# The first projection begins over half of its depth, and gate rows are spread by transfers through a line in DRAM

## The reference, cut to what matters

```python
mod = silu(c) @ w_mod[i] + b_mod[i]
sh1, sc1, g1, sh2, sc2, g2 = split(mod, 6)
h = rmsnorm(x, norm1_g) * (1 + sc1) + sh1
q, k, v, r = split(h @ w_in)          # gated linear attention, latents and context
x = x + g1 * y                        # gate 1
f = moe(rmsnorm(x, norm2_g) * (1 + sc2) + sh2)
x = x + g2 * f                        # gate 2
# second block: two layers (ab: two kinds of attention; cd: window attention and convolution)
h = rmsnorm(x) * (1 + scale) + shift
x = x + gate * mix(h)                 # a gate for latents, one for context in layer ab, one in layer cd
```

## Time and profile before

| | us |
|---|---|
| median of 3 runs | 1036.72 |
| lowest and highest run | 1036.17, 1038.57 |
| profiled execution, span from first to last instruction (it has no other time) | 1037.2 |
| TensorE matmuls busy | 953.9 |
| VectorE busy | 370.3 |
| ScalarE busy | 292.4 |
| GpSimd busy | 31.0 |

### The profile page before, as it was taken

The page is one execution under the profiler, slowest core; times in us unless marked ns, Lnnn a source line. Parts: engine busy times, 40 slices in busy tenths (PEclk is TensorE's granted clock), DMA queues, the critical chain, the costliest instruction groups (busy, mean ns, idle before and its releaser), DMA issues.

```text
span 1037.2 us, 11964 instructions
## 1 busy us (share of the span) xinstructions
PE 953.9 (92%) x4352; PEld 510.3 (49%) x4353; DVE 370.3 (36%) x876; ACT 292.4 (28%) x679; POOL 31.0 (3%) x53
## 2 busy tenths in 40 slices
PE   3899989999999889878877999999999999999998
PEld 1454446546444336323322655576454545676763
DVE  1200597624361000001000350485766423246452
ACT  3210543232322000000000341467666311225330
POOL 0100200000000000000000100000000000000000
PEclk8999999999999999999988999999999999999999
DMA  9955574489569999999999512205644104342411
GB/s 351 357 206 201 97 255 162 171 299 334 212 243 326 376 397 393 397 395 397 396 398 386 191 41 71 82 1 193 213 138 108 34 8 140 112 154 82 134 30 40
DMA packets 100750, 220.92 MB, mean 213 GB/s; under 512 B 2917, under 2 KB 5273, under 8 KB 100553
## 3 DMA queue, kind: packets, MB, share of 16 engines
q1 hardware_dynamic: 95520, 208.54, 55.9%
q0 software_dynamic: 2032, 6.84, 2.5%
q10 hardware_dynamic: 3128, 4.62, 1.2%
HBM read 214.48 MB, written 5.51 MB: 212 GB/s over the span
## 4 chain that ended last, share of the span: by engine, by line
PE 80%; DMA 8%; ACT 4%; SPq 3%; DVE 3%; issue 2%; ACTq 0%; DVEq 0%
PE bank L596 27%; PE bank L863 9%; PE bank L610 9%; DMA arena<-in_w_up_e_dram 5%; PE bank L876 4%; PE bank L893 4%; PE bank L1047 3%; PE bank L1066 3%; PE bank L562 3%; PE bank L888 3%; PE bank L1057 3%; DMA arena<-in_gla_w_in_dram 2%; SPq L1212 2%; PE bank L792 1%; SPq L1207 1%
## 5 line engine op out<-in xcount | busy, mean ns | idle before, releaser
L596 PE MATMUL bank<-arena 128*128 128x512 f32 (+3 forms) x672 | 269.9, 559 | 1.4 <-ACT arena L1443 0.7
L596 PEld LDWEIGHTS bank<-arena 128*128 128x128 f32 x672 | 125.9, 190 | 133.7 <-issue 124.1
L863 PE MATMUL bank<-arena 128*64 128x512 f32 x512 | 120.6, 625 | 13.1 <-issue 13.1
L610 PE MATMUL bank<-arena 128*128 128x256 f32 (+1 forms) x384 | 99.4, 417 | 4.0 <-DMA arena<-in_gla_w_in_dram 2.4
L610 PEld LDWEIGHTS bank<-arena 128*128 128x128 f32 x384 | 72.0, 190 | 32.2 <-issue 21.5
L863 PEld LDWEIGHTS bank<-arena 128*64 128x64 f32 x512 | 43.3, 144 | 87.0 <-issue 86.3
L876 PE MATMUL bank<-arena,con 128*64 128x512 f32 x272 | 62.1, 597 | 9.6 <-ACT con L1535 9.0
L562 PE MATMUL bank<-arena,silu_c 128*32 128x512 f32 x384 | 49.0, 633 | 8.4 <-DMA arena<-in_w_mod_dram 6.0
L1532 ACT ACTIVATE con<-bank 128x256 f32<-128x256 f32 x16 | 6.1, 384 | 177.6 <-PE bank L863 177.6
L2164 DVE TENSOR_TENSOR con<-con,bank 128x256 f32<-128x256 f32 x16 | 6.7, 420 | 135.4 <-ACT con L1532 135.4
L1047 PE MATMUL bank<-arena 64*128 64x512 f32 (+3 forms) x160 | 47.7, 545 | 2.2 <-ACT arena L1705 2.2
(11 more groups left out here) (351 smaller groups left out, 1067.7 us busy)
## 6 DMA issues: line engine op xcount, KB each, us to landing
arena<-in_w_gate_e_dram SPq DMA_DIRECT2D x16, 2048.0 KB, 20.0
arena<-in_w_up_e_dram SPq DMA_DIRECT2D x16, 2048.0 KB, 20.3
arena<-in_w_down_e_dram SPq DMA_DIRECT2D x16, 2048.0 KB, 19.8
arena<-in_w_mod_dram SPq DMA_DIRECT2D x12, 2048.0 KB, 11.8
arena<-in_mod_w_dram SPq DMA_DIRECT2D x12, 2048.0 KB, 8.5
arena<-in_gla_w_in_dram SPq DMA_DIRECT2D x6, 2048.0 KB, 10.8
arena<-in_ab_w_in_dram SPq DMA_DIRECT2D x6, 2048.0 KB, 16.4
arena<-in_cd_w_in_dram SPq DMA_DIRECT2D x6, 2048.0 KB, 7.8
```

Source lines behind the costliest of these rows:

```text
L596: mm = pe.matmul(ps[:, 0:n], lhs[:, k, tile * P:(tile + 1) * P], w[:, k, c0:c0 + n], start=(k == 0), stop=(k == kd_ - 1))
L610: mm = pe.matmul(ps[:, i * n:(i + 1) * n], w[:, k, c * P:(c + 1) * P], rhs[:, k, 0:n], start=(k == 0), stop=(k == KC - 1))
L863: mm = pe.matmul(up_b[64 * j:64 * j + 64, :], h[:, k, :], blocks[:, g + n:u + n + 1:u - g, :], start=(k == 0), stop=(k == KC - 1), tile_po ...
```

## The change

Two parts. **Front:** the chunks are made in the order 0, 2, 1, 3, so that after two of them shift and scale of the first four depth chunks are known. The key weights are loaded in two halves of the depth, the first behind the second modulation chunk, the second behind the fourth. TensorE turns depth chunks 0 to 3, and starts all four heads over that half, with modulation chunks and turns between; the four banks are held until the other half is added. **Gate rows:** the diagonals, matmuls and copies go; GpSimd's queue writes the columns as a line of 1024 values to DRAM, waits, and reads the line spread over the partitions.

```diff
+        gate_lines = nc.dram_tensor("gate_lines", [5, D], F32, kind="Internal").ap()
-        mod_chunks = [(0, c) for c in range(12)] + ...
+        mod_chunks = [(0, c) for c in (0, 2, 1, 3)] + [(0, c) for c in range(4, 12)] + ...
...
+            if m == 1:
+                for name, ks in (("k", slice(0, 4)), ("k_rest", slice(4, KC))):
+                    loads.append((name, [(slice(0, P), ks, cols_of(w_in, 512, 512)[:, ks, :])], 2, KC, 512))
+        loads.append(loads.pop(3))
-        FRONT_LOADS = [("k", 2), (4, 0), ("q", 1), (5, 0), ...
+        FRONT_LOADS = [(4, 0), ("q", 1), (5, 0), ...
...
-            for m in range(2):
-                mod(m)
-            turn(0, xn, range(0, 6))
-            banks.hold([f"turn0_{k}" for k in range(6)])
-            for m in range(2, 4):
-                mod(m)
+            mod(0)
+            turn(0, xn, range(0, 4))
+            mod(1)
             mod_flush()
+            def keys_part(h, ks):
+                w = weights(pe, "k")
+                if ks[0]:
+                    pe.wait_ge(k_rest_in, 16)
+                ps = banks.open(pe, f"k{h}", k_ready, h + 1) if ks[0] == 0 else banks.banks[banks.at[f"k{h}"][0]]
+                for k in ks:
+                    if h == 0:
+                        wait_turned(0, k)
+                    mm = pe.matmul(ps[:, :], w[:, k, h * P:(h + 1) * P], hT[:, k, :], start=(k == 0), stop=(k == KC - 1))
+                if ks[-1] == KC - 1:
+                    banks.filled(f"k{h}", mm)
+                    last_use["k"] = f"k{h}"
+            keys_part(0, range(0, 4))
+            keys_part(1, range(0, 4))
+            banks.hold(["k0", "k1"])
+            mod(2)
+            keys_part(2, range(0, 4))
+            banks.hold(["k2"])
+            mod(3)
+            turn(0, xn, range(4, 6))
+            mod_flush()
+            keys_part(3, range(0, 4))
+            banks.hold(["k3"])
+            turn(0, xn, range(6, KC))
             banks.give_back()
-            turn(0, xn, range(6, KC))
             for h in range(HG):
-                project_T(f"k{h}", "k", [h], 512, hT, k_ready, h + 1, turned=0 if h == 0 else None)
+                keys_part(h, range(4, KC))
                 if h == 1:
                     mod(4)
             mod(5)
...
-                if t == 0:
-                    gate(0)
...
-            ctx_latents(1)
-            gate(1)
-            ctx_latents(4)
+            ctx_latents(5)
+            pe.wait_ge(con_rest_in, 16)
             pe.wait_ge(routed, 1)
...
-                if m in AB_GATE_AT:
-                    gate(2 + AB_GATE_AT.index(m))
...
-            gate(4)
...
-            dve.wait_ge(gate_bc, 2)
+            dve.wait_ge(gate_row_in[0], 16)
...
+            def gate_row(u, col, targets):
+                line = gate_lines[u]
+                pool.dma_start(line.rearrange("(k p) -> p k", p=P), col, allow_slow_non_contiguous=True).then_inc(gate_line_out[u], 16)
+                pool.wait_ge(gate_line_out[u], 16)
+                for target, cs in targets:
+                    pool.dma_start(target, line[cs].partition_broadcast(target.shape[0])).then_inc(gate_row_in[u], 16)
+            pool.wait_ge(modcol_ready, 6)
+            gate_row(0, mod1[:, 16:24, 0], [(gate_rows[:, 0, :], slice(0, D))])
             banks.wait(pool, "z31")
...
+            pool.wait_ge(o_copied, 4)
+            pool.wait_ge(modcol_ready, 12)
+            gate_row(1, mod1[:, 40:48, 0], [(gate_rows[64 * h:64 * h + 64, 1, 0:512], slice(512 * h, 512 * h + 512))
+                                            for h in range(2)])
             banks.wait(pool, "col17")
...
+            pool.wait_ge(modcol_ready, 18)
+            pool.wait_ge(qk_ms, 8)
+            gate_row(2, mod2[:, 0, 16:24, 0], [(gate_rows[:, 0, :], slice(0, D))])
+            gate_row(3, mod2[:, 0, 16:24, 1], [(ctx_gate_row, slice(0, D))])
+            pool.wait_ge(modcol_ready, 24)
+            pool.wait_ge(y_added, 12)
+            gate_row(4, mod2[:, 1, 16:24, 0], [(gate_rows[:, 0, :], slice(0, D))])
```

More of the change, by code:

```diff
@@ L133, in hold @@
     def hold(self, names):
-        self.held = [self.at[x][0] for x in names]
+        self.held = self.held + [self.at[x][0] for x in names]
         self.order = [n for n in self.order if n not in self.held]
@@ L138, in give_back @@
         self.order += self.held
+        self.held = []
     def filled(self, name, ins):
@@ L328, in cols_of @@
             return w.rearrange("(k p) c -> p k c", p=P)[:, :, c0:c0 + n]
-        mod_chunks = [(0, c) for c in range(12)] + [(1, c) for c in range(6)] + [(2, c) for c in range(6)]
+        mod_chunks = [(0, c) for c in (0, 2, 1, 3)] + [(0, c) for c in range(4, 12)] + [(1, c) for c in range(6)] + [(2, c) for c in range(6)]
         w_in = a["gla_w_in"][0]
@@ L471, in build @@
         o_copied, o_rstd, o_ready, oT_ready = sem("o_copied"), sem("o_rstd"), sem("o_ready"), sem("oT_ready")
-        diag_gate, gate_bc, y_added = sem("diag_gate"), sem("gate_broadcast"), sem("y_added")
+        gate_line_out, y_added = [sem(f"gate_line{u}_out") for u in range(5)], sem("y_added")
+        gate_row_in = [sem(f"gate_row{u}_in") for u in range(5)]
         parts_zeroed, parts_copied = sem("parts_zeroed"), sem("parts_copied")
@@ L613, in project_T @@
                 last_use[wname] = name
[L615 to L630, removed]
             pe.wait_ge(con_in, 16)
@@ L1202, in fill @@
                 name, parts, s, kdim, n = ld
+                if name == "k_rest":
+                    rows, ks, src = parts[0]
+                    sp.dma_start(view(slot_at(s), kdim, n)[rows, ks, :], src).then_inc(k_rest_in, 16)
+                    return
                 if in_slot[s] is not None:
@@ L1316, in mod, with turn @@
                 act.activation(mod_rows[:, m % 2, :], ps[:, :], ACT.Copy).then_inc(row_ready, 1)
-            def turn(use, dst, cs, at=0):
-                act.wait_ge(coef_ready, max(c for _, _, c in cs) + 1)
-                for k in range(0, KC, 2):
+            def turn(use, dst, cs, at=0, ks=range(0, KC, 2), sem_=coef_ready):
+                act.wait_ge(sem_, max(c for _, _, c in cs) + 1)
+                for k in ks:
                     ps = banks.wait(act, f"turn{use}_{k}")
@@ L1326, in turn @@
                     ins.then_inc(turned_a, 1)
[L1328 to L1336, removed]
             act.wait_ge(cols_ready, 2)
@@ L1347, in _ @@
             norm(0, xn, arrived)
-            for m in range(4):
-                mod(m)
-            turn(0, hT, [(0, T, 0), (T, 512, 1)])
+            mod(0)
+            mod(1)
+            turn(0, hT, [(0, T, 0), (T, 512, 1)], ks=range(0, 4, 2), sem_=coef_first)
+            mod(2)
+            mod(3)
+            turn(0, hT, [(0, T, 0), (T, 512, 1)], ks=range(4, KC, 2))
             for h in range(HG):
@@ L1878, in turn @@
                     ins.then_inc(turned_v, 1)
-            def gate(u, col):
-                if u >= 1:
-                    banks.wait(dve, f"gate{u - 1}_1")
-                dve.tensor_tensor(gate_diag[:, :, :], outer(ident, KC), inner(col, P), ALU.mult).then_inc(diag_gate, 1)
             added = [0]
@@ L1902, in _ @@
             norm_rows(0, xn)
-            for m in range(4):
-                mod_col(m)
-            dve.wait_ge(modcol_ready, 4)
-            for m in range(2):
-                coefficients(m, mod1[:, 8:16, m], mod1[:, 0:8, m], column("norm1_g"))
-            turn(0, hT, [(0, T, 0), (T, 512, 1)])
+            for half, sem_ in ((0, coef_first), (1, coef_ready)):
+                mod_col(2 * half)
+                mod_col(2 * half + 1)
+                dve.wait_ge(modcol_ready, 2 * half + 2)
+                s4 = slice(4 * half, 4 * half + 4)
+                for m in range(2):
+                    coefficients(m, mod1[:, 8 + 4 * half:12 + 4 * half, m], mod1[:, 4 * half:4 * half + 4, m],
+                                 column("norm1_g")[:, s4], s4, sem_)
+                turn(0, hT, [(0, T, 0), (T, 512, 1)], ks=range(4 * half + 1, 4 * half + 4, 2), sem_=sem_)
             mod_col(4)
@@ L2390, in _ @@
             turn(5, hT, [(0, T, 5)])
-            gate(4, mod2[:, 1, 16:24, 0])
             for n, t in enumerate(CD_TILES):
```

43 lines of the change are left out of this document (18 added, 25 removed).

## The result

The change made the kernel slightly slower, by 0.2 to 0.4%. In the six runs beside six of the kernel before, the median is 1042.45 us (1038.68 to 1043.81) against 1037.09; ratio 1.0039, 95% interval 1.0028 to 1.0051. Twelve later runs of the same kernel (experiment 10) gave 1039.40 (1036.56 to 1041.96) and 1.0017 (1.0007 to 1.0028). The forecast was 1031.6, range 1030.0 to 1035.6. The profiled execution of the changed kernel took 1043.02 us with a span of 1041.2; in every run whose span is known the two differ by about 1.8. The runs of this document come in sets, from several chips, each with the kernel before beside it. One and the same kernel differed by up to 3.0 us from set to set (1042.45 and 1039.40 here), so a difference of that size between medians of different sets decides nothing.

What follows compares the result with a forecast made beforehand. TensorE's order was taken to bound the kernel, except the experts' stage, paced by the stream of weights. Front +0.8, second broadcast -0.7, third to fifth -5.16 sum to -5.1: median 1031.6 us, range 1030.0 to 1035.6.

Steps and rivals of the forecast that it cites:

- three signs: Forecast wrong if the gap's clock drops, the chunk after 715 waits for its load, or attention's turns begin no earlier.
- First broadcast, value 0: At 246.50, before the first output product: removal gains 0, since ScalarE's evictions still release the product at 248.60.
- rival 1: Clock falls in the 3.2 us gap before 248.60, slowing the product by 2.0: 1033.6; chance 0.22 alone.
- The line, 7.2 us and a stall of 0: After attention, near 697: each scattered line takes 7.2 us and delays the chunk wanted at 720.17 by 0.
- Rival 4: Scattered lines hold the DMA engines, making the chunk wanted at 720.17 late; up to 8.6 us, 1040.2; chance 0.07.
- Front, +0.8: Kernel start to the sixth chunk: the new order costs 0.8 us, bounds 0.4 to 1.8.
- the first two cases of the clock's rise: Front: clock rises at 25.8 as before, or 5.7 us after the restart; second chunk ends at 27.3 or 28.0.
- Rival 2: Clock falls in the front's 2.1 us gap before the first half of the keys, costing 2.0: 1033.6; chance 0.10 alone.
- Second broadcast, 0.7: Before the ranks' matmul at 296.11: removal gains 0.7 us, 0.55 sure, up to 1.0.
- Third to fifth, 5.16: Third, fourth (attention) and fifth broadcast: removal gains 1.72 us each, 5.16 together; upper bound 1.96 each.
- rival 3: ScalarE and VectorE set attention, so removing the third and fourth broadcast leaves holes: 2 x 1.72 less gain, 1035.0; chance 0.07.
- The experts' stage, "almost unmoved": The expert stage, paced by the stream of weights, begins +0.8 - 0.7 later, so almost unmoved.

Runs made afterwards that it cites:

- experiment 10: The whole change, unaltered, run once more beside the kernel before: 1039.40 us, ratio 1.0017.
- the pair: Whole change, third and fourth gate lines written at about 612 us, on one chip: with four throwaway matmuls in the first broadcast's gap 1032.36, without 1035.27.
- early lines: Against the whole change, third and fourth gate lines written to DRAM after the second context load, about 612 us: 1033.48, once more 1035.27.
- experiment 8: Front's edits alone, old gates, against 1037.25 before: unaltered 1040.69; sixth chunk in third chunk's buffer 1038.15; second chunk before first 16 transposes 1037.14.
- the rows alone, with early lines and fill: Gate rows by transfers, old front, third and fourth line written early, four throwaway matmuls in the first broadcast's gap: 1030.82, 0.9926 of the kernel before.

## Why the prediction was wrong

Two steps failed, and both are terms that the sum put at nothing: the line's stall of 0, which measured 7.30 us with the slow clock behind it, and the first broadcast's 0, which measured 2.95. Together they are 10.25 us. The forecast of -5.1 and the trace's +3.98 lie 9.0 apart: the front added 0.65 (1.45 at the first product, and not 0.8) and the second broadcast 0.2, while the other three broadcasts took 1.0 off and the experts' stage 1.06. Two of the three signs that the prediction named for its being wrong came: the clock dropped, and the chunk waited for its load.

**First broadcast, value 0: wrong.** That the product's start would not move was right (ScalarE's copies still release it). The step left out what the two matmuls did for the clock; it was kept apart as rival 1, at 2.0 us and 0.22. It happens in seven of eight profiles and makes the product up to 3.1 longer; the pair's medians differ by 2.9. The one wait that had stayed fast, of 2.43 us, was no guide to one of 3.18; the prediction's own rows had two falls, behind 2.23 and 2.9 us.

**The line, 7.2 us and a stall of 0: wrong, and the largest.** Rival 4 had the mechanism, at 0.07. The two lines took 10.4 to 13.2. The step's reason, that queues share the engines so that a load goes on beside a line, is what failed: the load moved at 6 to 32 GB/s. So did "only one of the two lines should meet that load": each waits for the one before it on GpSimd's queue, and both met it. The nearest rows were 1024 pieces of 64 bytes read from DRAM; 1024 pieces of 4 bytes written to it took 12.3 even in quiet, so the number of pieces alone doesn't set the time. The packet price of the Trainium skill, "DMA: Bandwidth & Descriptors", section "Measured", a figure for loads from DRAM, gave the prediction its estimate of 10.8 us; the 10.4 to 13.2 here lie about it, while the 3.0 of rows 9 for as many pieces doesn't fit it. The sum had not taken it.
Stall and slow clock cost 7.3 in the trace, 5.0 in the change's second profile; early lines took 4.1 to 9.0 off by the medians.

**Front, +0.8: mis-sized.** Its own bounds, 0.4 to 1.8, held in the trace (1.58), and each step was right to half a microsecond: second chunk's restart 25.1 forecast and 25.57 found, keys between 30.9 and 32.3 and found at 31.77, sixth chunk 68.0 to 69.4 and 69.14. The value lay between the first two cases of the clock's rise; the profile lies between the second and the third. By the medians the front costs 2.2 to 3.4; what makes up the rest is open (experiment 8). Rival 2 exists beside it: in three profiles with this front the first 16 half-depth passes took 8.80 us instead of 7.11. TensorE's timeline and stretches of one of them, the change's second profile (experiment 10):

```profile
21.65 3.63 PE L590 MATMUL bank<-con,arena 128*128 128x128 f32 x16 [5.20 <-DVE arena L1848]
25.21 1.92 PE L571 MATMUL bank<-arena,silu_c 128*32 128x512 f32 x16
...
30.56 8.80 PE L645 MATMUL bank<-arena 128*128 128x512 f32 x16 [2.05 <-ACT arena L1336]
```

```profile
29.00:31.00 2.00, 0.44 (x1) 0.30 (x2) 1.96 (x8) 1.61 (x4) 0.00 (x0) 1.00 1.05 388
31.00:36.00 5.00, 5.00 (x9) 2.11 (x8) 0.29 (x1) 0.33 (x1) 0.00 (x0) 0.66 1.05 387
```

The transposes, 0.23 us each, ran at the lower level and the second chunk at the higher; behind the gap of 2.05 the clock was still at 1.00 when the keys began, and fell after 31. There the sixth chunk is 2.30 late and not 1.58. Two readings of the prediction were off without touching its sum: the waits between 20.07 and 37.85 are 3.2 us and not about 4, and 1037.2 is a span, some 1.8 short of a time, so the profiled execution was 2.3 above the median of 1036.72 and not 0.5.

**Second broadcast, 0.7:** 0.50, about the part called sure.

**Third to fifth, 5.16: right in kind, too small.** 1.97 + 2.47 + 1.73 = 6.17, above the upper bound of three times 1.96. Besides the matmuls, short waits went: groups of TensorE in the stretch of the third and fourth of the kernel before,

```profile
L1057 PE MATMUL bank<-con,arena 128*128 128x128 f32 x60 | 8.5, 275 | 0.6 <-ACT arena L1705 0.5
```

and of the kernel with early lines,

```profile
L1068 PE MATMUL bank<-con,arena 128*128 128x128 f32 x60 | 8.1, 274 | 0.0
```

TensorE had waited 0.6 us at the turns, mostly for ScalarE, which had two evictions more to do there; that these are the cause is likely and not shown. The gain itself speaks against rival 3.

**The experts' stage, "almost unmoved":** 1.06 shorter in the change's profile. Since it varies by 3.9 between profiles without an edit in it, that can't be put down to the change; what sets it stays open.

With both faults repaired the forecast's reasoning about the broadcasts holds: the rows alone, with early lines and fill, are 7.4 us faster by the medians (1030.82 against 1038.17), of which the trace has 6.2 in the three large terms and 0.5 in the second.

## What to carry to other kernels

A step that idles an engine can be free for the order of work and still cost the clock: ask what ran in the gap. A transfer off the critical path is priced by its pieces and by what else is wanted while it runs; write scattered columns where no load is due, and look for a place hundreds of microseconds earlier. When work is moved ahead, check what the moved work waits for (here the normalized rows), since everything behind it inherits that wait.

## What the runs showed that was not expected

- A 4 KB line in 1024 pieces took 12.3 us (median of two) even in the quiet stretch behind 611 us, 2.6 as one piece; while such lines were under way, a 2 MB load on another queue moved 6 to 63 GB/s and landed after 21.4 us instead of 8.8.
- While the first line held the load, the DMA share in the records was only 0.06 to 0.44: the hold does not show as busy engines there. While the second held it, the share was 0.87.
- The same gap of 3.18 us was followed by a fall of the clock in seven profiles and not in the eighth; in the front of the change, eleven profiles have the first 16 transposes at the lower level's length (3.40 to 3.68 us). In five of them the clock had risen before and fell in the first gap. In six it had not risen yet, though the column of the granted clock has 1.00 there: only the length of the passes tells the level before its first record. In three of these six it fell after the second gap.
